# Expert weights in 2 MB units of four neighbouring rows per partition, in 8 ring slots instead of 16, with one more early unit

## The chip, the cores and the metric

The kernel runs on one core of one Trainium2 chip. The metric is the device time of one execution in microseconds (us); lower is better. The kernel before has a median of 1139.06 us over three runs (1138.79 to 1141.54).

## The reference

One layer of a streaming encoder on 256 tokens (and 16 learned ones in front), D = 1024, all in float32. A mixer of two head groups, a gated linear attention and a state-space model, comes first, then a mixture of 32 experts, each with three matrices of 1024 x 1024. Cut to what matters:

```python
mix = hybrid_mixer(h, w_in, ...)              # uses w_in (1024 x 3096) and w_out (1024 x 1024)
h = layer_norm(alpha * h + mix)
logits = h @ router_w + router_b              # top 4 of 32 experts per token
for e in range(32):                           # for the tokens x_e that chose expert e
    hid = clamped_swiglu(x_e @ w_gate[e] + b_gate[e], x_e @ w_up[e] + b_up[e])
    y_e = (hid @ w_down[e] + b_down[e]) * gate
h = layer_norm(alpha * h + sum over experts of y_e)
```

The weights of the experts are 32 x 3 x 4 MB = 384 MB (MB here is 1,048,576 bytes), and every expert's are read, whoever chose it.

## The kernel before

**Stages.** The mixer takes the first 165 us or so, the router the time to 193 us, the experts the rest. In the expert stage tokens are taken 64 at a time (a tile). `tile` (lines 946 to 992, TensorE) handles one expert:

- `hidden` for the gate matrix: the bias product of line 953, then line 959: for each of the eight row blocks `kt` of 128 rows, products of the 64 gathered tokens `xT` (the stationary operand, 64 columns) with 1024 columns of the matrix (the moving operand, two times 512). A float32 product is two instructions, so a matrix is 32 instructions.
- `scatter` of the expert before (line 942), `hidden` for the up matrix, then `gather` of the next expert's tokens (line 934): the stationary operand is a 128 x 128 piece of the token rows `xh`, read with a stride, the moving one a 0/1 matrix of 64 columns.
- four transposes of the hidden values (line 975, the same stride), two of the weights of the tokens (line 978), another `scatter`, and line 990: the down matrix.

**Weight units.** `unit_src` (line 241) cuts each matrix into four units of 256 rows. In a unit, partition p holds the rows 2p and 2p+1, which are neighbours in memory: one run of 8 KB per partition, 1 MB per unit, 12 units per expert (`UPE`). Since row 2p+k stands in partition p, the tokens have to be gathered in that order, and this is what `pair_rows` (line 254) does: for row block kt it takes every second column of `xh` or of `u_c`.

**Ring.** `ring` has 16 slots of 1 MB. The first 16 MB that it holds are the mixer's weights, 12 units of `w_in` in runs of 1 KB and 4 of `w_out`. From then on the slots are filled in order with expert units. SyncE issues all of it from one in-order program (`experts`, lines 306 to 337): before each DMA it waits until TensorE is done with the slot's last unit (for the first round the table `w_used` of line 299, afterwards the counters `unit_used`, `g_ps`, `u_ps` and `d_ps`, which TensorE raises after the eight instructions that use a unit), then issues the DMA at line 329. TensorE waits for a unit in `arrived` (line 1002).

**Early units.** The first four units of expert 28 (its gate matrix) don't pass through the ring. `load_spare` (line 302) puts them into four places in the working memory `arena` that the mixer no longer needs: two when the ring is at its thirteenth expert unit (line 318), and two after the sixteenth (line 332), one of these when the router's logits are done and one when the normalised tokens are no longer needed in transposed form. In the last round `ring_at` (line 258) skips them.

**Order of the rounds.** Four experts are written out in a loop body; the first and the last round stand outside the loop. Ahead of the last round, at expert 28, `add_residual` (line 921) adds eight products.

Of the kernel before, what the change touches and what calls it, by code (L numbers as in the profile page):

```python
# [12 lines left out]
P = 128  # L13
D = 1024
KT = D // P
# [25 lines left out]
RING = 16  # L41
UW = 2048
UPE = 3 * D * FF // (P * UW)
UNROLL = 4
ROUNDS = NE // UNROLL
SPARE = 4
# [9 lines left out]
def build(nc, x, meta, ln_in_g, ln_in_b, w_in, gla_w_a2, gla_b_a, gla_norm_g, ssd_conv_w, ssd_conv_b,  # L56
          ssd_dt_bias, ssd_a_log, ssd_d, ssd_norm_g, w_out, ln1_g, ln1_b, router_w, router_b,
          w_gate, w_up, b_gate, b_up, w_down, b_down, ln2_g, ln2_b, out):
    with ExitStack() as ctx:
# [7 lines left out]
        arena = sb("arena", [P, 19392])  # L67
# [56 lines left out]
        spare = [cut(at, 2, D) for at in (8320, 16576, 3072, 5248)]  # L124
# [77 lines left out]
        ln1_in, ln2_in, bias_in, late_in, out_done = sem("ln1_in"), sem("ln2_in"), sem("bias_in"), sem("late_in"), sem("out_done")  # L202
        landed = [sem(f"landed{s}") for s in range(RING)]
# [37 lines left out]
        def unit_src(e, u):  # L241
            m = (w_gate, w_up, w_down)[u // (UPE // 3)]
            q = u % (UPE // 3)
            rows = slice(q * 2 * P, (q + 1) * 2 * P)
            return m[0, e, rows, :].rearrange("(p k) n -> p (k n)", k=2) if isinstance(e, int) else \
                m[0, bass.ds(e, 1), rows, :].rearrange("a (p k) n -> p (a k n)", k=2)

        def slot(s):
            return ring[:, s, :].rearrange("p (k n) -> p k n", k=2)
# [17 lines left out]
        def _(sp):  # L267
# [9 lines left out]
            for n, c0 in enumerate(W_ORDER):  # L277
                sp.dma_start(ring[:, n, :].rearrange("p (k n) -> p k n", k=KT),
                             w_in[0, :, c0:c0 + 256].rearrange("(k p) n -> p k n", p=P)).then_inc(landed[n], 16)
# [14 lines left out]
            for n in range(4):  # L294
                sp.dma_start(ring[:, U_OUT + n, :].rearrange("p (k n) -> p k n", k=KT),
                             w_out[0, :, 256 * n:256 * n + 256].rearrange("(k p) n -> p k n", p=P)).then_inc(landed[U_OUT + n], 16)


            w_used = [(conv_ps, 2), (conv_ps, 4), (conv_ps, 6), (conv_ps, 8), (k_ps, 1), (v_ps, 3), (v_ps, 3), (q_ps, 1),
                      (half_used, 1), (z_ps, 2), (half_used, 2), (og_ps, 2), (wout_ps, 3), (wout_ps, 3), (wout_ps, 4), (wout_ps, 4)]  # L300

            def load_spare(q):
                sp.dma_start(unit_dst(spare[q]), unit_src(NE - UNROLL, q)).then_inc(spare_in, 16)

            def experts(it):
                first = isinstance(it, int) and it == 0
                for i in range(UPE * UNROLL):
                    at = ring_at(it, i)
                    if at is None:
                        continue  # L310
                    before = at - RING
                    if before >= 0:
                        before += i - at
                    if first and i == U_OUT:

                        sp.wait_ge(mixT_ps, 4)
                        load_spare(0)
                        sp.wait_ge(bparts_ok, 1)
                        load_spare(1)
                    if first and before < 0:  # L320
                        sp.wait_ge(*w_used[i])
                    else:
                        k, u = before // UPE, before % UPE
                        m, q = u // 4, u % 4
                        if q == 3:
                            sp.wait_ge((g_ps, u_ps, d_ps)[m], it * UNROLL + (k + 1))
                        else:
                            sp.wait_ge(unit_used, (it * UNROLL + k) * 9 + (3 * m + q + 1))
                    sp.dma_start(ring[:, at % RING, :], unit_src(it * UNROLL + i // UPE, i % UPE)).then_inc(landed[at % RING], 16)  # L329
                    if first and i == RING - 1:  # L330
                        sp.wait_ge(logit_ps, 1)
                        load_spare(2)
                        sp.wait_ge(h1_ok, NT)
                        load_spare(3)
# [4 lines left out]
            sp.wait_ge(g_ps, NE - UNROLL + 1)  # L339
# [269 lines left out]
        def _(pe):  # L609
# [9 lines left out]
            def wslot(n, kt, a=0, b=256):  # L619
                return ring[:, n, :].rearrange("p (k n) -> p k n", k=KT)[:, kt, a:b]  # L620
# [32 lines left out]
            for c in range(XC):  # L653
                n = U_XBC + c // 2
                pe.wait_ge(landed[n], 16)
# [30 lines left out]
            pe.wait_ge(landed[U_K], 16)  # L686
# [15 lines left out]
            pe.wait_ge(landed[U_V], 16)  # L702
# [28 lines left out]
            pe.wait_ge(landed[U_V + 1], 16)  # L731
# [25 lines left out]
            pe.wait_ge(landed[U_Q], 16)  # L757
# [36 lines left out]
            for hf in range(2):  # L794
                n = U_Z + hf
                pe.wait_ge(landed[n], 16)
# [45 lines left out]
            for hf in range(2):  # L842
                n = U_OG + hf
                pe.wait_ge(landed[n], 16)
# [12 lines left out]
            def out_part(t, kts, first):  # L857
                for nb in range(2):
                    b = bank[((1, 4), (2, 3))[t][nb]]
                    for kt in kts:  # L860
                        ins = mm(b[:, :], mixT[:, kt, t * P:(t + 1) * P],  # L861
                                 ring[:, U_OUT + 2 * nb:U_OUT + 2 * nb + 2, kt * 256:(kt + 1) * 256],
                                 start=first and kt == kts[0], stop=(not first) and kt == kts[-1], skip_group_check=True)
                    if not first:
                        ins.then_inc(wout_ps, 1)

            for n in range(4):
                pe.wait_ge(landed[U_OUT + n], 16)
# [60 lines left out]
            def gather(n, par):  # L929

                pe.wait_ge(sel_ok, n + 1)
                for kt in range(KT):
                    for t in range(NT):
                        ins = mm(bank[7][:, kt * SL:(kt + 1) * SL], pair_rows(xh[:, t, :], kt), sel[:, par, t, :], start=t == 0, stop=t == 1)  # L934
# [11 lines left out]
            def tile(n, par, first, unit_at, arrived, gathers, scatters):  # L946

                def hidden(m, b, free, done):
# [5 lines left out]
                    for q in range(4):  # L954
                        arrived(4 * m + q)
                        for k in range(2):
                            kt = 2 * q + k
                            for h in range(2):
                                ins = mm(b[h * SL:(h + 1) * SL, :], xT[par][:, kt, :], unit_at(4 * m + q)[:, k, h * 512:(h + 1) * 512],  # L959
                                         start=False, stop=kt == KT - 1)  # L960
                        ins.then_inc(done if q == 3 else unit_used, 1)
# [12 lines left out]
                for c in range(4):  # L974
                    ins = tr(bank[4][:, c * P:(c + 1) * P], pair_rows(u_c, c), ident[:, :])  # L975
# [9 lines left out]
                for q in range(4):  # L985
                    arrived(8 + q)
                    for k in range(2):
                        kt = 2 * q + k
                        for h in range(2):
                            ins = mm(bank[6][h * SL:(h + 1) * SL, :], hidT[:, kt % 4, (kt // 4) * SL:(kt // 4 + 1) * SL],  # L990
                                     unit_at(8 + q)[:, k, h * 512:(h + 1) * 512], start=kt == 0, stop=kt == KT - 1)
                    ins.then_inc(d_ps if q == 3 else unit_used, 1)

            def experts(it):
                for k in range(UNROLL):
                    def unit_at(u):
                        at = ring_at(it, UPE * k + u)
                        return spare[u] if at is None else slot(at % RING)

                    def arrived(u):  # L1000
                        at = ring_at(it, UPE * k + u)
                        if at is None:
                            pe.wait_ge(spare_in, 16 * SPARE)
                        else:

                            pe.wait_ge(landed[at % RING], it * (UPE * UNROLL // RING * 16) + (2 + at // RING) * 16)
# [16 lines left out]
            with pe.If(nx > 0):  # L1023
                with pe.Fori(0, nx) as i:
                    gather(i + NE, 0)
                    def arrived(u):

                        uses = 1 + (NE * UPE - SPARE + RING - 1 - u) // RING
                        pe.wait_ge(landed[u], i * 16 + (uses + 1) * 16)
                    tile(i + NE, 0, False, slot, arrived, False, False)  # L1030
# [347 lines left out]
```

## Time and profile before

| | |
|---|---|
| median of three runs | 1139.06 us |
| the profiled execution | 1139.48 us |
| its span, first to last instruction | 1137.6 us |
| mean granted TensorE clock | 0.984 of full speed |
| TensorE busy | 1095.9 us (96%) |
| VectorE, ScalarE, GpSimd busy | 231.1, 123.7, 30.7 us |
| moved by DMA | 426.96 MB (here and in all rows: million bytes), mean 375 GB/s |

The profiled execution took 1.9 us more than its span and 0.4 us more than the median. Busy shares of TensorE are modelled from pipelined instructions and don't show short waits between them; where the time goes is read from the chain of waits and from the DMA rows.

### The profile page before, as it was taken

The numbers are of one execution on the slowest core, as the hardware profiler recorded it, in microseconds if no ns is written. First come the engines' busy times: TensorE is split into PE (matmuls) and PEld (weight loads), VectorE is DVE, ScalarE is ACT, GpSimd is POOL, SyncE is SP. The second block draws the span as 40 slices with busy tenths as digits, with TensorE's granted clock in tenths as the row PEclk, the third lists the DMA queues.
The fourth block names the chain that finished last, engine by engine and source line by source line (L and its number), as shares of the span: only waits on it lengthen the run. The fifth ranks groups of instructions, "written<-read, shape, count | busy, mean of one in ns | idle before, by whom it ended". The sixth has DMA issues, their size and how long they took to land.

```text
span 1137.6 us, 13806 instructions
## 1 busy us (share of the span) xinstructions
PE 1095.9 (96%) x5600; PEld 517.9 (46%) x5600; DVE 231.1 (20%) x528; ACT 123.7 (11%) x250; POOL 30.7 (3%) x37
## 2 busy tenths in 40 slices
PE   6999998999999999999999999999999999999994
PEld 5787756444444444444444433333333333344441
DVE  4422464011111111111111111111111111111114
ACT  2241422000000000000000000000000000000001
POOL 0230002000000000000000000000000000000000
PEclk9989997899999999999999999999999999999998
DMA  8973534899999999999999999999999999999992
GB/s 260 353 302 125 170 150 157 349 411 422 421 421 420 421 421 422 421 422 421 422 422 422 422 422 422 421 423 421 422 421 423 421 422 422 422 422 421 422 419 87
DMA packets 78240, 426.96 MB, mean 375 GB/s; under 512 B 10537, under 2 KB 27026, under 8 KB 29058
## 3 DMA queue, kind: packets, MB, share of 16 engines
q1 hardware_dynamic: 76082, 423.83, 91.4%
q10 hardware_dynamic: 2128, 2.70, 0.9%
q8 instruction: 22, 0.36, 0.1%
q14 instruction: 8, 0.07, 0.0%
HBM read 425.46 MB, written 1.05 MB: 375 GB/s over the span
## 4 chain that ended last, share of the span: by engine, by line
PE 66%; DMA 29%; DVE 2%; ACT 2%; SPq 1%; issue 0%; DVEq 0%
DMA ring<-in_moe_w_up 28%; PE bank L959 26%; PE bank L990 13%; PE bank L934 7%; PE bank L942 4%; PE bank L659 3%; PE bank L861 2%; PE bank L847 1%; PE bank L799 1%; SPq L329 1%; PE bank L953 1%; PE bank L975 1%; PE bank L735 1%; PE bank L675 1%; PE bank L761 1%; PE bank L682 0%
## 5 line engine op out<-in xcount | busy, mean ns | idle before, releaser
L959 PE MATMUL bank<-ring,arena 128*64 128x512 f32 x2016 | 452.7, 596 | 13.6 <-DMA ring<-in_moe_w_up 13.6
L959 PEld LDWEIGHTS bank<-ring,arena 128*64 128x64 f32 x2016 | 139.7, 137 | 294.4 <-issue 234.5
L990 PE MATMUL bank<-ring,arena 128*64 128x512 f32 x1024 | 231.1, 604 | 0.0
L990 PEld LDWEIGHTS bank<-ring,arena 128*64 128x64 f32 x1024 | 71.7, 139 | 156.2 <-issue 137.0
L934 PEld LDWEIGHTS bank<-arena 128*128 128x128 f32 x1024 | 126.2, 200 | 25.1 <-issue 25.1
L934 PE MATMUL bank<-arena 128*128 128x64 f32 x1024 | 130.4, 287 | 0.0
L1303 DVE COPY arena<-bank 128x512 f32<-128x512 f32 x32 | 22.1, 692 | 346.3 <-PE bank L990 346.3
L1294 DVE TENSOR_SCALAR arena<-bank 128x512 f32<-128x512 f32 x32 | 22.1, 692 | 261.9 <-PE bank L959 261.9
L942 PE MATMUL bank<-arena 64*128 64x512 f32 x256 | 72.2, 642 | 0.9 <-DVE arena L1303 0.9
L576 ACT ACTIVATE arena<-arena 128x512 f32<-128x512 f32 x32 | 20.2, 631 | 465.8 <-DVE arena L1290 465.8
L1290 DVE TENSOR_SCALAR arena<-bank 128x512 f32<-128x512 f32 x32 | 22.1, 692 | 186.9 <-PE bank L959 186.9
L572 ACT ACTIVATE arena<-bank 128x512 f32<-128x512 f32 x32 | 19.1, 598 | 362.1 <-PE bank L934 362.1
L942 PEld LDWEIGHTS bank<-arena 64*128 64x128 f32 x256 | 19.4, 184 | 32.5 <-issue 32.5
L659 PE MATMUL bank<-arena,ring 128*128 128x272 f32 x128 | 30.4, 393 | 0.7 <-ACT arena L436 0.7
L861 PE MATMUL bank<-ring,arena 128*128 128x512 f32 x64 | 27.9, 593 | 0.9 <-ACT arena L430 0.9
L953 PE MATMUL bank<-arena 96*64 96x512 bf16 x128 | 25.7, 396 | 0.8 <-ACT arena L572 0.8
L659 PEld LDWEIGHTS bank<-arena,ring 128*128 128x128 f32 x128 | 23.8, 190 | 5.5 <-ACT arena L436 0.9
L975 PE MATMUL bank<-ident,arena 128*128 128x128 f32 x128 | 21.7, 292 | 2.2 <-DVE arena L1299 2.2
L1299 DVE SCALAR_TENSOR_TENSOR arena<-arena 128x512 f32<-128x512 f32 x32 | 22.2, 693 | 3.3
L953 PEld LDWEIGHTS bank<-arena 96*64 96x64 bf16 x128 | 7.3, 108 | 34.0 <-issue 34.0
L1296 DVE TENSOR_TENSOR arena<-arena 128x512 f32<-128x512 f32 x32 | 21.8, 681 | 0.0
L975 PEld LDWEIGHTS bank<-ident,arena 128*128 128x128 f32 x128 | 19.1, 218 | 3.1 <-DVE arena L1299 3.1
(242 smaller groups left out, 527.0 us busy)
## 6 DMA issues: line engine op xcount, KB each, us to landing
ring<-in_moe_w_up SPq DMA_DIRECT2D x128, 1024.0 KB, 26.2
ring<-in_moe_w_down SPq DMA_DIRECT2D x128, 1024.0 KB, 26.3
ring<-in_moe_w_gate SPq DMA_DIRECT2D x124, 1024.0 KB, 25.7
ring<-in_w_in SPq DMA_DIRECT2D x12, 1024.0 KB, 11.9
ring<-in_w_out SPq DMA_DIRECT2D x4, 1024.0 KB, 13.7
arena<-in_moe_w_gate SPq DMA_DIRECT2D x4, 1024.0 KB, 4.7
arena<-in_x SPq DMA_DIRECT2D x2, 512.0 KB, 4.7
arena<-in_ln_in_g SPq DMA_DIRECT2D x1, 512.0 KB, 10.0
```

The source lines that it names most:

```text
L659: ins = mm(bank[4 + c % 3][:, 3:3 + TOK], wslot(n, kt, (c % 2) * P, (c % 2) * P + P), hT[:, kt, :], start=kt == 0, stop=kt == KT - 1)
L861: ins = mm(b[:, :], mixT[:, kt, t * P:(t + 1) * P], ring[:, U_OUT + 2 * nb:U_OUT + 2 * nb + 2, kt * 256:(kt + 1) * 256], start=first and k ...
L934: ins = mm(bank[7][:, kt * SL:(kt + 1) * SL], pair_rows(xh[:, t, :], kt), sel[:, par, t, :], start=t == 0, stop=t == 1)
L942: ins = mm(bank[2 * t + h][:, :], selGT[h * SL:(h + 1) * SL, t * P:(t + 1) * P], y_s[h * SL:(h + 1) * SL, :], start=False, stop=False, ski ...
L953: mm(b[h * SL:(h + 1) * SL, :], oh[:, par, :], bparts[:, m, h * 512:(h + 1) * 512], start=True, stop=False)
L959: ins = mm(b[h * SL:(h + 1) * SL, :], xT[par][:, kt, :], unit_at(4 * m + q)[:, k, h * 512:(h + 1) * 512], start=False, stop=kt == KT - 1)
L975: ins = tr(bank[4][:, c * P:(c + 1) * P], pair_rows(u_c, c), ident[:, :])
L990: ins = mm(bank[6][h * SL:(h + 1) * SL, :], hidT[:, kt % 4, (kt // 4) * SL:(kt // 4 + 1) * SL], unit_at(8 + q)[:, k, h * 512:(h + 1) * 512 ...
L1290: ts(a_c, bank[4][:, :], LIMIT, None, ALU.min).then_inc(a_ok, 1)
L1294: ts(u_c, bank[5][:, :], LIMIT, -LIMIT, ALU.min, ALU.max).then_inc(u_ok, 1)
L1299: stt(u_c, u_c, 1.0, a_c, ALU.add, ALU.mult).then_inc(hid_ok, 1)
L1303: copy(y_s, bank[6][:, :]).then_inc(yd_ok, 1)
```

## The change

`UW` goes from 2048 to 4096 float32 per partition, `RING` from 16 to 8, so the ring keeps its 16 MB. A matrix is now two units of 2 MB (`UPM` = 2, `UPE` = 6). In a unit, partition p holds the rows 4p to 4p+3, one run of 16 KB. `spread_rows` takes the place of `pair_rows` and takes every fourth column. The units of the mixer's weights stay at 1 MB, two to a slot, with semaphores of their own; a slot is free for its first expert unit when both halves are used.

The scratch room that the compiler keeps for DMA descriptors is set to 1 KB per partition, and `arena` grows by 16 KB per partition. The early units are now three of 2 MB (`SPARE` = 3: the gate matrix of expert 28 and the first half of its up matrix), loaded as six halves of 1 MB in runs of 8 KB. The first two halves go to the new room of `arena` and are issued straight behind `w_out`; the four others go where the early units were, at the same points of the program.

```diff
-RING = 16
-UW = 2048
+RING = 8
+UW = 4096
+HW = UW // 2
+RPP = UW // FF
 UPE = 3 * D * FF // (P * UW)
+UPM = UPE // 3
-SPARE = 4
+SPARE = 3
-        arena = sb("arena", [P, 19392])
+        arena = sb("arena", [P, 19392 + UW])
-        spare = [cut(at, 2, D) for at in (8320, 16576, 3072, 5248)]
+        spare = [cut(at, 2, D) for at in (19392, 19392 + HW, 8320, 16576, 3072, 5248)]
...
+            m, q = (w_gate, w_up, w_down)[u // UPM], u % UPM
+            rows = slice(q * RPP * P, (q + 1) * RPP * P)
+            return m[0, e, rows, :].rearrange("(p k) n -> p (k n)", k=RPP) if isinstance(e, int) else \
+                m[0, bass.ds(e, 1), rows, :].rearrange("a (p k) n -> p (a k n)", k=RPP)
+        def half_src(e, u, j):
...
+            return m[0, e, rows, :].rearrange("(p j k) n -> p j (k n)", j=2, k=RPP // 2)[:, j, :]
...
-        def pair_rows(v, kt):
-            return v.rearrange("p (q s k) -> p q k s", s=P, k=2)[:, kt // 2, kt % 2, :]
+        def spread_rows(v, kt):
+            return v.rearrange("p (q s k) -> p q k s", s=P, k=RPP)[:, kt // RPP, kt % RPP, :]
...
+            w_used = [((conv_ps, 4),), ((conv_ps, 8),), ((k_ps, 1), (v_ps, 3)), ((q_ps, 1),), ((z_ps, 2),), ((og_ps, 2),),
+                      ((wout_ps, 3),), ((wout_ps, 4),)]
+            load_spare(0)
+            load_spare(1)
...
-                    if first and i == U_OUT:
+                    if first and i == U_OUT // 2:
                         sp.wait_ge(mixT_ps, 4)
-                        load_spare(0)
+                        load_spare(2)
                         sp.wait_ge(bparts_ok, 1)
-                        load_spare(1)
+                        load_spare(3)
...
-                    for q in range(4):
-                        arrived(4 * m + q)
-                        for k in range(2):
-                            kt = 2 * q + k
+                    for q in range(UPM):
+                        arrived(UPM * m + q)
+                        for k in range(RPP):
+                            kt = RPP * q + k
...
-                        ins.then_inc(done if q == 3 else unit_used, 1)
+                        ins.then_inc(done if q == UPM - 1 else unit_used, 1)
...
-    nc = bacc.Bacc("TRN2", target_bir_lowering=False, num_devices=1)
+    nc = bacc.Bacc("TRN2", target_bir_lowering=False, num_devices=1, dynamic_dma_scratch_size=1024)
```

## Rows read from the trace of the kernel before

**Rows 1.** The page, part 2: the span in 40 slices of 28.4 us.

```profile
DMA  8973534899999999999999999999999999999992
GB/s 260 353 302 125 170 150 157 349 411 422 421 421 420 421 421 422 421 422 421 422 422 422 422 422 422 421 423 421 422 421 423 421 422 422 422 422 421 422 419 87
```

**Rows 2.** The page, part 4: the chain that ended last, by engine.

```profile
PE 66%; DMA 29%; DVE 2%; ACT 2%; SPq 1%; issue 0%; DVEq 0%
```

**Rows 3.** The same chain in order of time: start us, us, what.

```profile
227.97 6.87 PE bank L959 x32
236.24 6.87 PE bank L959 x32
...
256.05 6.87 PE bank L959 x32
...
664.94 26.97 DMA ring<-in_moe_w_up
...
721.79 1.96 PE bank L959 x8
724.59 26.99 DMA ring<-in_moe_w_up
...
965.23 27.39 DMA ring<-in_moe_w_up
994.60 3.91 PE bank L934 x32
...
1007.32 3.63 PE bank L925 x8
1011.29 6.87 PE bank L959 x32
...
1103.77 6.90 PE bank L959 x32
```

**Rows 4.** Busy time by window: PE, PEld, DVE, ACT, POOL, granted clock, DMA share, GB/s.

```profile
85.00:90.00 5.00, 5.00 (x36) 3.26 (x36) 0.00 (x0) 0.65 (x2) 0.00 (x0) 1.00 0.00 0
190.00:195.00 5.00, 4.22 (x18) 3.09 (x19) 0.00 (x0) 1.88 (x2) 0.00 (x0) 0.50 0.00 0
215.00:220.00 5.00, 5.00 (x12) 1.51 (x12) 0.00 (x0) 0.00 (x0) 0.00 (x0) 0.68 0.68 283
220.00:225.00 5.00, 5.00 (x16) 1.37 (x14) 0.00 (x0) 0.00 (x0) 0.00 (x0) 0.64 0.47 169
240.00:300.00 60.00, 60.00 (x315) 25.54 (x312) 9.42 (x22) 4.25 (x8) 0.00 (x0) 1.00 1.01 422
```

**Rows 5.** Timeline of SyncE's queue, 220 to 229 us: start us, us issuing, count.

```profile
221.51 0.33 SPq L329 DMA_DIRECT2D ring<-in_moe_w_gate  x1
224.37 0.33 SPq L329 DMA_DIRECT2D ring<-in_moe_w_gate  x1
226.08 2.04 SPq L329 DMA_DIRECT2D ring<-in_moe_w_gate  x2
```

**Rows 6.** The DMA view of 30 to 45 us (1 KB runs), then of 240 to 1000 us.

```profile
DMA packets 5182, 5.22 MB, mean 348 GB/s; under 512 B 80, under 2 KB 5182, under 8 KB 5182
...
DMA packets 44003, 320.52 MB, mean 422 GB/s; under 512 B 4887, under 2 KB 4887, under 8 KB 4887
```

**Rows 7.** Timeline of TensorE: contiguous transposes, then the gather with its stride of two.

```profile
178.01 2.16 PE L617 MATMUL bank<-ident 128*128 128x128 f32 x18
...
243.04 3.98 PE L934 MATMUL bank<-arena 128*128 128x64 f32 x32
```

**Rows 8.** The page, part 5: weight loads of 64 and of 128 columns; the gather's matmul.

```profile
L959 PEld LDWEIGHTS bank<-ring,arena 128*64 128x64 f32 x2016 | 139.7, 137 | 294.4 <-issue 234.5
L934 PE MATMUL bank<-arena 128*128 128x64 f32 x1024 | 130.4, 287 | 0.0
L659 PEld LDWEIGHTS bank<-arena,ring 128*128 128x128 f32 x128 | 23.8, 190 | 5.5 <-ACT arena L436 0.9
```

More of the change, by code:

```diff
@@ L202, in build @@
         ln1_in, ln2_in, bias_in, late_in, out_done = sem("ln1_in"), sem("ln2_in"), sem("bias_in"), sem("late_in"), sem("out_done")
+        w_landed = [sem(f"w_landed{n}") for n in range(16)]
         landed = [sem(f"landed{s}") for s in range(RING)]
@@ L241, in unit_src, with w_unit @@
         def unit_src(e, u):
[L242 to L246, printed above, removed]
+            m, q = (w_gate, w_up, w_down)[u // UPM], u % UPM
[3 more added lines that the diff above has]
+        def half_src(e, u, j):
+            m, q = (w_gate, w_up, w_down)[u // UPM], u % UPM
+            rows = slice(q * RPP * P, (q + 1) * RPP * P)
+            return m[0, e, rows, :].rearrange("(p j k) n -> p j (k n)", j=2, k=RPP // 2)[:, j, :]
         def slot(s):
-            return ring[:, s, :].rearrange("p (k n) -> p k n", k=2)
+            return ring[:, s, :].rearrange("p (k n) -> p k n", k=RPP)
+        def w_unit(n):
+            return ring[:, n // 2, (n % 2) * HW:(n % 2 + 1) * HW].rearrange("p (k n) -> p k n", k=KT)
         def unit_dst(v):
             return v.rearrange("p k n -> p (k n)")
-        def pair_rows(v, kt):
-            return v.rearrange("p (q s k) -> p q k s", s=P, k=2)[:, kt // 2, kt % 2, :]
+        def spread_rows(v, kt):
+            return v.rearrange("p (q s k) -> p q k s", s=P, k=RPP)[:, kt // RPP, kt % RPP, :]
         def ring_at(it, i):
@@ L277, in _ @@
             for n, c0 in enumerate(W_ORDER):
-                sp.dma_start(ring[:, n, :].rearrange("p (k n) -> p k n", k=KT),
-                             w_in[0, :, c0:c0 + 256].rearrange("(k p) n -> p k n", p=P)).then_inc(landed[n], 16)
+                sp.dma_start(w_unit(n), w_in[0, :, c0:c0 + 256].rearrange("(k p) n -> p k n", p=P)).then_inc(w_landed[n], 16)
                 if n == 3:
@@ L294, in _, with load_spare @@
             for n in range(4):
[L295 to L303, printed above, removed]
+                sp.dma_start(w_unit(U_OUT + n), w_out[0, :, 256 * n:256 * n + 256].rearrange("(k p) n -> p k n", p=P)).then_inc(w_landed[U_OUT + n], 16)
+            w_used = [((conv_ps, 4),), ((conv_ps, 8),), ((k_ps, 1), (v_ps, 3)), ((q_ps, 1),), ((z_ps, 2),), ((og_ps, 2),),
+                      ((wout_ps, 3),), ((wout_ps, 4),)]
+            def load_spare(h):
+                sp.dma_start(unit_dst(spare[h]), half_src(NE - UNROLL, h // 2, h % 2)).then_inc(spare_in, 16)
+            load_spare(0)
+            load_spare(1)
             def experts(it):
@@ L331, in experts @@
                         sp.wait_ge(logit_ps, 1)
[L332 removed]
+                        load_spare(4)
                         sp.wait_ge(h1_ok, NT)
[L334 removed]
+                        load_spare(5)
             experts(0)
@@ L619, in wslot @@
             def wslot(n, kt, a=0, b=256):
-                return ring[:, n, :].rearrange("p (k n) -> p k n", k=KT)[:, kt, a:b]
+                return w_unit(n)[:, kt, a:b]
             pe.wait_ge(consts, 3)
@@ L654, in _ @@
                 n = U_XBC + c // 2
-                pe.wait_ge(landed[n], 16)
+                pe.wait_ge(w_landed[n], 16)
                 if c >= 3:
@@ L683, in meta_rows @@
                 return ins
-            pe.wait_ge(landed[U_K], 16)
+            pe.wait_ge(w_landed[U_K], 16)
             pe.wait_ge(conv, 7)
@@ L700, in _ @@
             ins.then_inc(la_ps, 1)
-            pe.wait_ge(landed[U_V], 16)
+            pe.wait_ge(w_landed[U_V], 16)
             pe.wait_ge(conv, 8)
@@ L730, in _ @@
             ins.then_inc(D_ps, 1)
-            pe.wait_ge(landed[U_V + 1], 16)
+            pe.wait_ge(w_landed[U_V + 1], 16)
             n = U_V + 1
@@ L755, in _ @@
                 ssd_update(c)
-            pe.wait_ge(landed[U_Q], 16)
+            pe.wait_ge(w_landed[U_Q], 16)
             pe.wait_ge(v_ok, 1)
@@ L795, in _ @@
                 n = U_Z + hf
-                pe.wait_ge(landed[n], 16)
+                pe.wait_ge(w_landed[n], 16)
                 for t in range(NT):
@@ L843, in _ @@
                 n = U_OG + hf
-                pe.wait_ge(landed[n], 16)
+                pe.wait_ge(w_landed[n], 16)
                 for t in range(NT):
@@ L861, in out_part @@
                         ins = mm(b[:, :], mixT[:, kt, t * P:(t + 1) * P],
-                                 ring[:, U_OUT + 2 * nb:U_OUT + 2 * nb + 2, kt * 256:(kt + 1) * 256],
+                                 ring[:, U_OUT // 2 + nb, :].rearrange("p (a k n) -> p a k n", a=2, k=KT)[:, :, kt, :],
                                  start=first and kt == kts[0], stop=(not first) and kt == kts[-1], skip_group_check=True)
@@ L867, in _ @@
             for n in range(4):
-                pe.wait_ge(landed[U_OUT + n], 16)
+                pe.wait_ge(w_landed[U_OUT + n], 16)
             pe.wait_ge(mixT_act, 2)
@@ L933, in gather @@
                     for t in range(NT):
-                        ins = mm(bank[7][:, kt * SL:(kt + 1) * SL], pair_rows(xh[:, t, :], kt), sel[:, par, t, :], start=t == 0, stop=t == 1)
+                        ins = mm(bank[7][:, kt * SL:(kt + 1) * SL], spread_rows(xh[:, t, :], kt), sel[:, par, t, :], start=t == 0, stop=t == 1)
                 ins.then_inc(gath_ps, 1)
@@ L984, in tile, with unit_at @@
                 pe.wait_ge(hidT_ok, n + 1)
[L985 to L988, printed above, removed]
+                for q in range(UPM):
+                    arrived(2 * UPM + q)
+                    for k in range(RPP):
+                        kt = RPP * q + k
                         for h in range(2):
                             ins = mm(bank[6][h * SL:(h + 1) * SL, :], hidT[:, kt % 4, (kt // 4) * SL:(kt // 4 + 1) * SL],
-                                     unit_at(8 + q)[:, k, h * 512:(h + 1) * 512], start=kt == 0, stop=kt == KT - 1)
-                    ins.then_inc(d_ps if q == 3 else unit_used, 1)
+                                     unit_at(2 * UPM + q, k)[:, h * 512:(h + 1) * 512], start=kt == 0, stop=kt == KT - 1)
+                    ins.then_inc(d_ps if q == UPM - 1 else unit_used, 1)
             def experts(it):
                 for k in range(UNROLL):
-                    def unit_at(u):
+                    def unit_at(u, r):
                         at = ring_at(it, UPE * k + u)
-                        return spare[u] if at is None else slot(at % RING)
+                        return spare[2 * u + r // 2][:, r % 2, :] if at is None else slot(at % RING)[:, r, :]
                     def arrived(u):
@@ L1002, in arrived @@
                         if at is None:
-                            pe.wait_ge(spare_in, 16 * SPARE)
+                            pe.wait_ge(spare_in, 16 * 2 * SPARE)
                         else:
-                            pe.wait_ge(landed[at % RING], it * (UPE * UNROLL // RING * 16) + (2 + at // RING) * 16)
+                            pe.wait_ge(landed[at % RING], it * (UPE * UNROLL // RING * 16) + (1 + at // RING) * 16)
                     n = it * UNROLL + k
@@ L1026, in arrived @@
                     def arrived(u):
-                        uses = 1 + (NE * UPE - SPARE + RING - 1 - u) // RING
+                        uses = (NE * UPE - SPARE + RING - 1 - u) // RING
                         pe.wait_ge(landed[u], i * 16 + (uses + 1) * 16)
-                    tile(i + NE, 0, False, slot, arrived, False, False)
+                    tile(i + NE, 0, False, lambda u, r: slot(u)[:, r, :], arrived, False, False)
                     for t in range(NT):
```

15 lines of the change are left out of this document (8 added, 7 removed).

## The prediction

> **What bounds the kernel now.** I read the slices first. From slice 9 to the last but one, DMA runs at 420 to 423 GB/s and its share is full [rows 1]; TensorE is busy there too, so the slices can't tell which of them sets the end. The chain can: 29% of it is DMA [rows 2]. In order of time it falls into three stretches [rows 3]. Up to about 630 us it is TensorE alone: gate matrices start at 227.97 and 256.05, so an expert costs TensorE 28.08 us. From 635 to 992 us nearly all of it is landings of up units. Two of these, two experts apart, are at 664.94 + 26.97 = 691.91 and 724.59 + 26.99 = 751.58, so 12 units take 29.84 us and one takes 2.486 us: DMA is 1.76 us slower per expert than TensorE, and the 16 MB in the ring cover this until 630 us. The last landing of the chain is that of expert 27's last up unit, at 965.23 + 27.39 = 992.62. From there on it is TensorE again, since expert 28's gate units came early.
>
> How much would a faster DMA give at most? With TensorE alone, expert 28's gate would start at 227.97 + 27 x 28.08 + 3.63 (line 925) = 989.8; it starts at 1011.29 [rows 3]. So 21.5 us are to be had, and no more. The end moves one for one with the landing at 992.62, as long as the delay stays above zero. I take it apart into a start, a number of units and a price. Sixteen expert units are in the ring when streaming begins, and expert 27's last up unit is number 27 x 12 + 8 = 332: 316 units are streamed, 316 x 2.486 = 785.6 us.
>
> **Longer runs.** The trace has full DMA stretches with two sizes of packet [rows 6]. At 30 to 45 us (5182 - 80) / 16 = 319 packets of 1 KB per engine took 15 us, 47.0 ns each; at 240 to 1000 us (44003 - 4887) / 16 = 2445 packets of 8 KB took 760 us, 310.8 ns each. The line through both has 0.0368 ns per byte and 9.4 ns per packet. A 16 KB packet would take 612.4 ns, against 621.6 for two of 8 KB: 1.5% less. A MB becomes 2.449 us instead of 2.486, and 316 MB cost **11.8 us less**. This goes beyond the sizes that the trace shows. The bounds: nothing, if the 422 GB/s are a limit of another kind (or the runs are cut at 8 KB), and 316 x 8 x 9.4 ns = 23.8 us if the constant vanished. I take the line, since it is the value between the two that both rows support.
>
> Of DMA the Trainium skill (DMA: Bandwidth & Descriptors, "Why small descriptors are slow") says that the engine spends about 3 fixed cycles per packet and that this matters for small ones, at 256 B; at 8 KB it would be 3 in 259 and the change would give some 0.6% of the streaming time, an estimate of about 4.6 us instead of 11.8, and the sum below would be 1140.6. The same page puts the ceiling of the fabric at 435 GB/s; the slope above, times 16 engines, comes to the same figure.
>
> **Coarser slots, at the start.** DMA is idle at 190 to 195 us, and again within 215 to 225 us, where it moves 283 and 169 GB/s [rows 4]: every slot is full, and SyncE waits for expert 0's down matrix, on which TensorE works at half clock. The first two quarters come free for issues at 221.51 and 224.37 [rows 5]. The stream as a whole starts at the issue time less the time of the units before it: 221.51 - 8 x 2.486 = 201.6, 224.37 - 9 x 2.486 = 202.0, 226.08 - 10 x 2.486 = 201.2; the latest counts, 202.0. With 2 MB slots the first down unit is free only when both quarters are: 224.37 - 4 x 4.898 = 204.8. So the start is **2.8 us later**. By 240 us the rate is 422 [rows 4], so no later gap.
>
> **Coarser units, at the end.** After a landing TensorE had 8 instructions to do, 1.96 us [rows 3]; now 16, half of a 6.87 us matrix plus the same start: 3.7 us. **1.7 us more**, once, behind expert 27's up matrix. In the experts before it this is hidden, as DMA goes on meanwhile: 7 of 8 slots are in flight then.
>
> **Stride of four instead of two.** This touches `gather` (32 instructions) and line 975 (4). The spacing of its instructions is set by the 128-column loads. Contiguous: (2.16 - 0.28) / 17 = 111 ns; stride two: (3.98 - 0.28) / 31 = 119 ns [rows 7] (0.28 us, about the 287 ns of one [rows 8], is the duration of the last). A stride of two costs 8 ns per load. No row shows a stride of four. Bounds: nothing, and one more full read of the columns; loads of 64 and 128 columns differ by 190 - 137 = 53 ns [rows 8], so 106 ns more for each of 36 loads, 3.8 us per expert. I take another 8 ns, nearest to the row: 0.3 us per expert. It counts where TensorE sets the pace: four gathers behind expert 27's up, **1.2 us**. Before them it is under the DMA.
>
> **Edits at nothing.** The early unit more: 2 MB, 5 us of DMA, put into the queue ahead of the first expert unit; idle time such as 85 to 90 us [rows 4] takes it. It doesn't shorten the stream up to expert 27, as it belongs to expert 28. Behind it there was slack already: expert 31's last up unit landed at about 992.62 + 44 x 2.486 = 1102.0 and was needed at 1103.77 + 5.15 = 1108.9 [rows 3]. The slack grows by 5 us and nobody waits for it; without that cover it would be worth those 5 us. The descriptor scratch: all weight DMAs are SyncE's; I find no user, cost from 0 to 0. Half as many issues and waits: SyncE and `arrived` are not late; 0. The slots' merged first waits (slot 2 on `v_ps`): all of them are in before tile 0, as the idle 190 to 195 shows; 0, and if one were late it would delay tile 0 by the 5 us of a unit at most.
>
> **Sum.** -11.8 + 2.8 + 1.7 + 1.2 = -6.1 us on the profiled 1139.5 gives 1133.4; the median stands 0.4 below the profiled execution: **1133.0 us**. The landing would be at 983.6, and of the 21.5 us of delay some 12.5 remain, less what the gathers take from it.
>
> **Rivals.**
>
> (a) *The gather becomes the bound.* Without DMA waits the end is 1139.5 - 21.5 + 32p, with p the added TensorE time per expert. At p = 0.67 us this is the time of before: 19 ns per load. With p = 3.8 it is 1240 us, 8.9% slower. For it: the loads are the bound of the gather already, and stride two is 8 ns dearer than none. Against: that is only 7%, at twice as many places in memory touched. The Trainium skill (SBUF — State Buffer, the note on cachelines under the port swizzle) says that lines have 16 bytes and that two hits per line are wanted to hide the access; a stride of four float32 has one. By that rule this rival holds. A load takes 0.83 ns per column (53 / 64 [rows 8]) while a moving operand takes 6.87 / 32 / 512 = 0.42, so a load has twice the time per line; this is why I give it only 0.2.
>
> (b) *Longer runs give nothing.* 422 GB/s stays: 1139.5 + 2.8 + 1.7 + 1.2 = 1145.2, median 1144.8, 0.5% slower. It includes the case that the packets are cut at 8 KB. The point from which it decides is a gain of 5.7 us, half of the line's. For it: the rate is flat to 1% in all slices. Chance 0.15.
>
> (c) *In between*: p from 0.55 to 0.75 us (1139.5 - 21.5 + 32p = 1135.6 to 1142), or a third to two thirds of the line's gain (4 to 8 us: 1141.2 to 1137.2). Some 1136 to 1142 us, chance 0.13. The skill's estimate above would fall here.
>
> (d) *More than the line gives*, down to the floor without any DMA wait, 1139.5 - 21.5 + 32 x 0.3 = 1127.6: chance 0.05.
>
> The forecast has 0.47, with 1129 to 1135.5 as its own range. **Numbers.** A measurement of this kernel tells about 0.3%, 3.4 us, from no change. Faster: forecast, (d) and a little of (c), 0.55. Same: most of (c), 0.13. Slower: (a), (b), 0.32. The range goes from 1128 over (b) and the lower part of (a), to 1160.
>
> **What would show it.** Right: 16 KB packets, about 51,000 packets in all instead of 78,240; slices at 428 GB/s; the chain's last DMA landing near 984 us; expert 28's gate about 7 us earlier than 1011.29; the gather at 4.0 to 4.3 us instead of 3.98. Wrong: slices at 422 (b); a gather of over 4.7 us and a chain with no DMA behind 250 us (a); a DMA gap of more than 5 us at 215 to 235 us; the last DMA landing of the chain behind expert 28.

## The result and the profile after

The changed kernel takes **1306.5 us** (median of four runs, 1304.1 to 1309.8) against 1139.4 for the kernel before on the same chips: a ratio of 1.1465, 95% interval 1.1433 to 1.1496, 167 us slower. The forecast was 1133.0, the range up to 1160. The page of the changed kernel, lines of parts 1 to 5:

```profile
span 1302.2 us, 13282 instructions
...
PEclk9989987899999888888888888888899999888888
DMA  8963556898988888888888888898998888856850
GB/s 272 358 261 135 161 194 258 357 383 369 374 367 368 367 367 366 363 367 366 365 364 368 365 366 365 365 379 380 387 382 364 366 367 367 365 236 255 369 248 33
DMA packets 51023, 426.94 MB, mean 328 GB/s; under 512 B 7513, under 2 KB 24002, under 8 KB 26034
...
PE 96%; DVE 2%; ACT 1%; DMA 0%; issue 0%; DVEq 0%
...
L947 PEld LDWEIGHTS bank<-arena 128*128 128x128 f32 x1024 | 241.4, 328 | 25.3 <-issue 25.3
...
L947 PE MATMUL bank<-arena 128*128 128x64 f32 x1024 | 247.3, 411 | 0.0
```

The packets are as announced, 51,023. Nothing else is as forecast. DMA has gone from the chain (0%, it was 29% [rows 2]), and its rate in the slices has fallen from 422 GB/s [rows 1] to about 367: it no longer sets the pace, the ring is full and DMA waits for TensorE. The gather, line 947 here, is busy for 247 us in all instead of 130, 411 ns per instruction instead of 287 [rows 8]. And the granted clock averages 0.904, where it was 0.984. One expert in the chain that ended last (start us, us, what):

```profile
744.74 6.87 PE bank L972 x32
751.61 1.06 PE bank L955 x4
752.67 0.34 PE bank L966 x2
753.00 6.87 PE bank L972 x32
759.87 7.66 PE bank L947 x32
767.53 0.85 PE bank L988 x4
768.39 0.43 PE bank L991 x2
768.81 2.01 PE bank L955 x4
770.82 7.83 PE bank L1003 x32
...
778.87 6.87 PE bank L972 x32
```

Gate matrices start at 744.74 and 778.87, 34.13 us apart instead of 28.08 [rows 3]. The gate and up matrices take 6.87 us as they did. The same part of an expert in the kernel before, in its chain: the gather, the two groups of transposes, the second scatter and the down matrix:

```profile
299.25 3.91 PE bank L934 x32
303.16 0.51 PE bank L975 x4
303.67 0.22 PE bank L978 x2
303.89 1.06 PE bank L942 x4
304.95 7.02 PE bank L990 x32
```

So of the 6.05 us (6.06 by these rounded rows), 3.75 are the gather. 0.21 + 0.95 + 0.81 = 1.97 are instructions that the change doesn't touch: they run after the clock has fallen. So do the four transposes of the hidden values, which the change does touch; question 5 shows that their 0.34 is the clock too and not the stride, which makes 2.31 us of clock. Windows of 1 us within the gather (columns as in [rows 4]):

```profile
763.00:764.00 1.00, 1.00 (x6) 1.00 (x6) 0.00 (x0) 0.00 (x0) 0.00 (x0) 1.00 0.96 410
766.00:767.00 1.00, 1.00 (x6) 1.00 (x5) 0.00 (x0) 0.00 (x0) 0.00 (x0) 0.50 0.92 393
```

In the first the clock is at its upper level (2.4 GHz), in the second at the lower one (1.2 GHz); it falls about 6 us into the slow loads and comes back in the down matrix. The gather itself does as many instructions per us at either level, so it isn't the clock that slows it. Nor is it DMA traffic beside it: the very first gather of the changed kernel, at 184.92 us, takes 7.68 us although DMA moves nothing from 188 us on; in the kernel before it took 6.73, both at a clock of about 0.5.

### The profile page after: what moved, and what is told of

Same layout as the page of the kernel before. It is cut to its first block, busy times and chain, and to the rows that moved or that the text cites. A ratio compares the mean times of both kernels' runs of the same rounds, so it can differ in the third digit from the quotient of the medians.

```text
span 1302.2 us, 13282 instructions
## 1 busy us (share of the span) xinstructions
PE 1273.3 (98%) x5600; PEld 658.9 (51%) x5600; DVE 231.0 (18%) x528; ACT 126.3 (10%) x250; POOL 30.7 (2%) x37
## 4 chain that ended last, share of the span: by engine, by line
PE 96%; DVE 2%; ACT 1%; DMA 0%; issue 0%; DVEq 0%
PE bank L972 34%; PE bank L1003 19%; PE bank L947 19%; PE bank L955 7%; PE bank L672 2%; PE bank L874 2%; PE bank L988 2%; PE bank L966 1%; PE bank L860 1%; PE bank L812 1%; PE bank L991 1%; PE bank L748 1%; PE bank L930 1%; PE bank L774 1%; PE bank L688 1%; PE bank L695 0%
## 5 line engine op out<-in xcount | busy, mean ns | idle before, releaser
L972 PE MATMUL bank<-ring,arena 128*64 128x512 f32 x2000 | 442.3, 595 | 0.0
L972 PEld LDWEIGHTS bank<-ring,arena 128*64 128x64 f32 x2000 | 141.1, 137 | 269.7 <-issue 265.0
L947 PEld LDWEIGHTS bank<-arena 128*128 128x128 f32 x1024 | 241.4, 328 | 25.3 <-issue 25.3
L1003 PE MATMUL bank<-ring,arena 128*64 128x512 f32 x1024 | 250.3, 644 | 0.0
L947 PE MATMUL bank<-arena 128*128 128x64 f32 x1024 | 247.3, 411 | 0.0
L1003 PEld LDWEIGHTS bank<-ring,arena 128*64 128x64 f32 x1024 | 75.1, 150 | 194.7 <-issue 194.7
L955 PE MATMUL bank<-arena 64*128 64x512 f32 x256 | 101.0, 877 | 0.9 <-DVE arena L1316 0.9
L955 PEld LDWEIGHTS bank<-arena 64*128 64x128 f32 x256 | 25.8, 244 | 37.6 <-issue 37.6
L988 PE MATMUL bank<-ident,arena 128*128 128x128 f32 x128 | 33.9, 418 | 2.2 <-DVE arena L1312 2.2
L988 PEld LDWEIGHTS bank<-ident,arena 128*128 128x128 f32 x128 | 28.2, 256 | 3.1 <-DVE arena L1312 3.1
## 6 DMA issues: line engine op xcount, KB each, us to landing
ring<-in_moe_w_up SPq DMA_DIRECT2D x63, 2048.0 KB, 11.6
```

Of the source, the lines that this page charges most:

```text
L947: ins = mm(bank[7][:, kt * SL:(kt + 1) * SL], spread_rows(xh[:, t, :], kt), sel[:, par, t, :], start=t == 0, stop=t == 1)
L955: ins = mm(bank[2 * t + h][:, :], selGT[h * SL:(h + 1) * SL, t * P:(t + 1) * P], y_s[h * SL:(h + 1) * SL, :], start=False, stop=False, ski ...
L988: ins = tr(bank[4][:, c * P:(c + 1) * P], spread_rows(u_c, c), ident[:, :])
```

## The experiments

The theory after reading this profile, **S**: reading the stationary operand with a stride of four columns doubles the load, and the clock falls behind it; the rest of the change does what the prediction said. The rival **D**: the 16 KB runs or the 2 MB slots slow TensorE or the transfers. Six questions, nine runs.

**1. The change without its stride.** In the changed kernel:

```diff
-            return v.rearrange("p (q s k) -> p q k s", s=P, k=RPP)[:, kt // RPP, kt % RPP, :]
+            return v.rearrange("p (q s k) -> p q k s", s=P, k=2)[:, kt // 2, kt % 2, :]
```

> The changed kernel with one edit: the stationary operands of the gather and of the hidden values' transposes are read with a stride of two columns again, as before the change, instead of four. (The tokens' columns then no longer go with the rows of the 2 MB units, so the products are of other pairs.) Theory S (the stride of four doubles the 128-column loads, and the clock falls behind them; nothing else in the change costs much): the gather is back at 3.98 us, the clock at 0.98, and the time is what the prediction's other terms give, 1139.5 - 11.8 + 2.8 + 1.7 = 1132 us, 1129 to 1136. Rival D (the 16 KB runs or the 2 MB slots slow TensorE or the transfers themselves): most of the 167 us stays, over 1200 us. Rival of the packets: slices stay at 422 GB/s and the time is about 1144 us.

Measured: 1128.8 us, ratio 0.9915 (0.9900 to 0.9929), 9.8 us faster than the kernel before (six runs from 1127.3 to 1131.2; the profiled one is the 1131.2). The slices of its page, and its chain around expert 28:

```profile
GB/s 261 353 343 151 126 167 193 297 415 424 428 428 427 428 427 427 429 428 428 428 428 429 427 429 429 429 428 429 428 428 429 428 429 428 429 427 428 428 364 38
```

```profile
949.14 35.18 DMA ring<-in_moe_w_up
...
984.36 3.65 PE bank L972 x16
988.02 3.91 PE bank L947 x32
...
1004.70 6.87 PE bank L972 x32
```

428 GB/s, and the last landing at 949.14 + 35.18 = 984.3. S stands, D falls: with the 16 KB runs and the 2 MB slots in place, the loss of 167 us is gone. (What the slots alone cost, some 3 us, is in question 6.)

**2. The stride without the change.** In the kernel before, `pair_rows` takes every fourth column:

```diff
-            return v.rearrange("p (q s k) -> p q k s", s=P, k=2)[:, kt // 2, kt % 2, :]
+            return v.rearrange("p (q s k) -> p q k s", s=P, k=4)[:, kt // 4, kt % 4, :]
```

> The kernel before with one edit: the same operands are read with a stride of four columns (again products of other pairs), units, slots and runs as before. Theory S: TensorE alone sets the pace, 34.1 us per expert as in the changed kernel, gather 7.7 us, clock about 0.90, 1295 to 1310 us. Rival D: the stride costs little by itself, under 1180 us.

Measured: 1305.4 us, ratio 1.1464 (1.1447 to 1.1481), the same ratio as the change. Its page and the end of its chain:

```profile
PEclk9989987889888888888888888888999999888888
```

```profile
1246.93 7.66 PE bank L934 x32
1255.87 2.01 PE bank L942 x4
1257.88 7.79 PE bank L990 x32
```

One line of address pattern accounts for all of the loss.

**3. No stride at all.** The changed kernel with `return v[:, kt * P:(kt + 1) * P]`.

> The changed kernel with those operands read without any stride (products of other pairs). Theory S, with DMA setting the pace: TensorE saves a further 8 ns on each of 36 loads in the four experts behind the last DMA wait, about 1 us less than with a stride of two: 1129 to 1135 us, a gather of 3.6 to 3.8 us. If TensorE rather than DMA sets the pace with a stride of two, it saves some 9 us against that run instead.

Measured: 1126.3 us, ratio 0.9893 (0.9878 to 0.9907), 2.5 us less than with a stride of two and below the 1129 to 1135 expected. Gather 3.71 us in its chain. It still waits for DMA up to expert 27 (last landing 980.3), so TensorE doesn't set the pace. The landing is 4.0 us earlier than in the run with a stride of two, and the traces show where 3.0 of these arise: at the start of the stream. There expert 0's down matrix takes 7.02 us at full clock instead of 9.90 at mostly half clock, and the first down unit is free for the issue at 222.19 us instead of 225.16. That the contiguous loads keep the clock up there isn't shown; both profiled runs without a stride have the 7.02, the four with a stride of two (the kernel before among them) 8.31 to 9.90.

**4. Which strides are slow?** One kernel, each expert of the unrolled loop with a stride of its own; the indices are `v[:, kt:kt + 127 * s + 1:s]`:

```diff
+                if step == 0:
+                    for kt in range(KT):
+                        for t in range(NT):
+                            ins = mm(bank[7][:, kt * SL:(kt + 1) * SL], strided(xh[:, t, :], kt, 1), sel[:, par, t, :], start=t == 0, stop=t == 1)
...
```

> The kernel before, with the gather's stationary operand read at a stride of 1, 2, 3 and 4 columns by position in the unrolled loop of four experts (products of other pairs; the transposes keep their stride of two). Theory S1, two reads per line of 16 bytes are enough: 3.6, 3.98, then a step; a stride of three (on average 1.33 reads per line) takes two thirds or all of the way to 7.5 us. Theory S2, cost by bytes stepped over: steady growth, 3.7, 4.0, 5.8, 7.6. Theory S3, only strides of 16 bytes and more are slow: a stride of three is as short as two, about 4.0, and four is 7.5. As one expert in four has the slow gather, the whole takes about 1150 us.

Measured, in one execution: 1193.4 us. The 32 instructions of the gather in its chain, strides 2, 3, 4 and 1 in this order:

```profile
486.00 3.95 PE bank L942 x32
...
514.10 6.06 PE bank L946 x32
...
546.72 7.66 PE bank L950 x32
...
580.90 3.72 PE bank L938 x32
```

The first loads of strides three and four in its timeline, at full clock:

```profile
514.89 1.49 PEld L946 LDWEIGHTS bank<-arena 128*128 128x128 f32 x8
...
546.86 1.26 PEld L950 LDWEIGHTS bank<-arena 128*128 128x128 f32 x5
```

At a stride of three two of them take 0.44 us in the timeline and eight take 1.49, so they are (1.49 - 0.44) / 6 = 175 ns apart; at a stride of four two take 0.56 us and five 1.26, so (1.26 - 0.56) / 3 = 233 ns. In lines of 16 bytes the four strides touch 32, 64, 96 and 128 per load. 64, 96 and 128 lines at 1.83 ns are 117, 176 and 234 ns; the contiguous load, 32 lines, stays at 111, 0.87 ns for each of its 128 columns. None of S1, S2 and S3 had this law; S2 comes nearest for strides up to four. (The 6.06 us at a stride of three include a stretch at half clock; 32 loads at 175 ns are 5.6.) The whole time was above the 1150 expected, for two reasons: the stride of three is slow too, and I had left out the clock, which in the chain falls behind the strides of three and four and not behind one and two. There it adds some 2.4 us each time (down matrix, second scatter and both groups of transposes), 38 us in all if it does so in every round, an estimate.

A second kernel separates lines from bytes, and asks whether the moving operand suffers too:

> The kernel before with two probes (products of other pairs; the residual's eight instructions ahead of the last round are replaced). First, the gather's stationary operand at strides of 5, 6, 7 and 8 columns by position in the loop. The runs so far gave 111, 118, 175 and 234 ns per load at strides of 1 to 4: the last three are 64, 96 and 128 lines of 16 bytes times 1.83 ns. Theory L (a read costs 1.83 ns per line, or 0.83 ns per column where that is more): all four strides read 128 lines, 234 ns each at full clock. Rival B (cost by the bytes stepped over): 290 to 470 ns. Second, a moving operand of 512 columns at strides of 1, 2 and 4 (lines 924, 926, 928), four products of two instructions each, spaced 213 ns at a stride of 1. Theory L: 256 and 512 lines, 470 and 940 ns per instruction. Rival M (only weight loads suffer): 213 ns for all three.

Its gathers in the timeline of TensorE, strides 6, 7, 8 and 5:

```profile
520.77 7.40 PE L944 MATMUL bank<-arena 128*128 128x64 f32 x32
554.84 7.65 PE L948 MATMUL bank<-arena 128*128 128x64 f32 x32
589.06 7.88 PE L952 MATMUL bank<-arena 128*128 128x64 f32 x32
623.36 7.31 PE L940 MATMUL bank<-arena 128*128 128x64 f32 x32
```

Eight instructions each with a moving operand of 512 columns at strides 1, 2 and 4:

```profile
1154.14 3.70 PE L924 MATMUL bank<-arena,tri 128*128 128x512 f32 x8
1157.67 3.76 PE L926 MATMUL bank<-arena,tri 128*128 128x512 f32 x8
1161.28 7.36 PE L928 MATMUL bank<-arena,tri 128*128 128x512 f32 x8
```

Strides of five to eight cost about what four does (7.2 to 7.8 us in the chain against 7.66, where a cost by bytes would have given 9.3 us and more): it is lines, not bytes, and theory L holds. It doesn't explain the 8% by which these four strides differ. The moving operand suffers too, so rival M falls. Less the duration of the last one (0.59, 0.61 and 1.06 us) and over seven gaps, they are 444, 450 and 900 ns apart, where L gave 470 and 940 for strides of two and four. My base was wrong there: 213 ns is about the spacing with a stationary operand of 64 columns (32 in 6.87 us), and with 128 columns it is 444 ns, probably because the two halves of 64 are worked on side by side, which no run tests. A stride of two costs 2% and a stride of four doubles, 1.76 ns per line.

**5. Loads and clock apart.** The changed kernel, gather cut in two:

```diff
+                if gathers:
+                    gather(n + 1, 1 - par, range(0, 4))
                 hidden(1, bank[5], u_ok, u_ps)
                 if gathers:
-                    gather(n + 1, 1 - par)
+                    gather(n + 1, 1 - par, range(4, 8))
```

> The changed kernel, whole computation, stride of four, with the gather cut in two: its first 16 products ahead of the up matrix and its last 16 behind it. It tells the two costs of the slow loads apart. If the fall of the clock comes from the 7.5 us of slow loads in one piece, it goes: 28.07 + 32 x (0.234 - 0.118) + 4 x 0.11 = 32.2 us per expert, the clock at 0.98 and 1139.5 - 21.5 + 32 x 4.15 = 1251 us. If the clock falls all the same, 1290 us or more.

Measured: 1281.6 us (1270.5 to 1283.0), ratio 1.1235 (1.119 to 1.128), mean clock 0.947 instead of 0.904. The up matrix (32 instructions), the transposes of the hidden values and the half gathers in two neighbouring experts of its timeline:

```profile
710.19 9.60 PE L973 MATMUL bank<-ring,arena 128*64 128x512 f32 x32
...
723.50 0.68 PE L991 MATMUL bank<-ident,arena 128*128 128x128 f32 x4
...
740.55 3.95 PE L947 MATMUL bank<-arena 128*128 128x64 f32 x16
...
744.67 7.03 PE L973 MATMUL bank<-ring,arena 128*64 128x512 f32 x32
751.63 3.94 PE L947 MATMUL bank<-arena 128*128 128x64 f32 x16
```

It lies between the two expectations. Cutting the slow stretch in two spares 25 us, and since the loads are the same I put all of it down to the clock. But the clock still falls in most experts, in 13 of the 15 between 414 and 900 us in the chain, for a shorter time and not always in the same place (in the first line, 9.60 instead of 7.03 us, it is in the up matrix). What decides when it falls was not settled.

Since the fall moves about, this run also shows the four transposes with their stride of four at full clock, the second line: 0.68 us. In the first probe of question 4, where they have a stride of two, the same four take 0.68 us at full clock (489.78 us) and 1.06 at half clock (519.96 us). So the stride of four costs the transposes nothing that is seen here, and the 0.34 us of the changed kernel are the clock. Without them the first expectation is 4 x 0.11 x 32 = 14 us lower, 1237; the measured time stays between the two.

**6. The other terms.** The coarser slots without the longer runs: the whole computation, two DMAs with 8 KB runs per slot, `pair_rows` as before.

```diff
-                    sp.dma_start(ring[:, at % RING, :], unit_src(it * UNROLL + i // UPE, i % UPE)).then_inc(landed[at % RING], 16)
+                    for j in range(2):
+                        sp.dma_start(ring[:, at % RING, j * HW:(j + 1) * HW], half_src(it * UNROLL + i // UPE, i % UPE, j)).then_inc(landed[at % RING], 16)
```

> 2 MB slots as in the change, but each is filled by two DMAs of 1 MB in runs of 8 KB, two rows per partition, and the operands have a stride of two: the whole computation is done. It has the coarser slots without the longer runs. By the prediction's terms: slices at 422 GB/s and 2.8 + 1.7 = 4.5 us more than the kernel before, 1143 us; against the run with stride two and 16 KB runs (1128.8), 11.8 us more, 1140.6. Rival: the coarser slots are what brought the 9.8 us, and it stays near 1129 us.

Measured: 1141.5 us, ratio 1.0029 (1.0017 to 1.0042), 3.3 us more than before. Page, and the chain at the last landing:

```profile
GB/s 262 355 333 148 138 171 173 332 422 422 421 421 421 420 422 422 422 421 422 422 420 423 422 421 422 422 422 422 422 422 422 421 422 423 421 422 421 421 391 38
```

```profile
994.65 3.65 PE bank L969 x16
```

422 GB/s again, and the landing 2.0 us later than the 992.62 of before [rows 3]. The slots cost, and the runs give: against the run with a stride of two it lands 10.3 us later, and takes 10.3 us more by the profiled executions, 12.7 by the medians.

The third early unit: run 1 with `SPARE = 2`.

> The run with a stride of two (1128.8 us) with two early units instead of three, in the four old places. Prediction: the third one serves expert 28's up matrix, for which nobody waits: the same to within 1 us, 1128 to 1130. Rival: it shortens the stream, and without it the time is 2.45 x 2 = 4.9 us longer, about 1133.7 us.

Measured: 1131.0 us, ratio 0.9929 (0.9909 to 0.9949), 1 us above the 1128 to 1130 expected. The interval overlaps that of the run with three, and the last landing is at 983.86 instead of 984.32. The early unit doesn't shorten the stream; by the two intervals a difference in the end of up to some 4 us can't be excluded, though the lowest and the highest of the six times (1127.6 and 1132.0) are only 0.3 and 0.8 us above those of the other six.

**A version that keeps the gain.** The order of the columns can be put right once, instead of at each load:

```diff
+                for q in range(2):
+                    ins = nc.scalar.activation(xp[:, t, q * 512:(q + 1) * 512].rearrange("p (k s) -> p k s", k=RPP),
+                                               xh[:, t, q * 512:(q + 1) * 512].rearrange("p (s k) -> p k s", k=RPP), ACT.Copy)
...
-                stt(u_c, u_c, 1.0, a_c, ALU.add, ALU.mult).then_inc(hid_ok, 1)
+                stt(hp.rearrange("p (k s) -> p s k", k=RPP), u_c.rearrange("p (s k) -> p s k", k=RPP), 1.0,
+                    a_c.rearrange("p (s k) -> p s k", k=RPP), ALU.add, ALU.mult).then_inc(hid_ok, 1)
```

> 2 MB units and 16 KB runs as in the change, but the columns are put in the order of the rows once: ScalarE copies the tokens' rows into a permuted buffer before the first gather, and VectorE writes the hidden values permuted, so both kinds of load read contiguous columns. The early units are two again, since the buffer takes the new room. The whole computation is done. Theory S (only the strided loads cost): the time of the run without stride, 1126.3, plus at most 2 us for the copy ahead of the first gather: 1125 to 1130 us. Rival: VectorE's strided write or the copy on ScalarE is slow enough to be waited for (hidden values later than the gather, first gather later): 1131 us or more.

Measured: **1126.4 us**, ratio 0.9898 (0.9881 to 0.9916), 1.0% faster than the kernel before with the whole computation. Its chain behind the last landing, and VectorE's permuted write in its groups by line:

```profile
982.57 3.65 PE bank L979 x16
986.22 3.72 PE bank L954 x32
989.94 0.44 PE bank L995 x4
```

```profile
L1319 DVE SCALAR_TENSOR_TENSOR arena<-arena 128x512 f32<-128x512 f32 x32 | 33.7, 1054 | 3.3
```

The permuted write takes 1054 ns instead of 693, and ScalarE's copies took 1.1 us each for 512 columns; the first gather starts at 188.1 us in its chain, 2.3 us later than in the kernel before. The permuted write is covered by the gather: the transposes (line 995) start at 989.94, when it ends. The copies don't show in the medians (1126.4 against 1126.3 with no stride and no copy), but they do in the profiled executions: the first down unit is issued at 224.82 instead of 222.19, the last landing is at 982.52 instead of 980.30, and the end is 2.6 us later. A copy that is done before the first gather needs it would be worth up to that.

## Why the prediction was wrong

- **The failed step** is "Stride of four instead of two", in its words: "I take another 8 ns, nearest to the row: 0.3 us per expert." Measured: 115 ns more per load of the gather, 3.75 us for its 32, and nothing for the transposes; and that in every expert, since TensorE then sets the pace throughout, and not in four of them. The upper bound that I had put there, one more full read of the columns, 106 ns, was nearly exact (its 3.8 us are for 36 loads, of which only the 32 of the gather turned out slower). I extended two points (111 and 119 ns at strides one and two) as if the cost grew with the stride. It is the larger of two limits, one per column and one per line, and the second overtakes the first just below a stride of two: the 8 ns were not a small slope but the foot of a steep one.
- **Rival (a)** is what happened, with a chance of 0.2. Its price of 1240 us was the loads' alone. Here the forecast lacked a second mechanism altogether: the clock falls behind the slow loads in nearly every expert, 2.31 us of other work per expert. The sum with the measured terms is 1139.5 - 21.5 + 32 x (3.75 + 2.31) = 1312, against 1304.1 for the profiled execution. It counts 32 full experts, where the last has no gather and the clock falls less in the first ones and in the last (down matrices of 7.02 to 7.49 us in experts 1 to 3, 7.04 in expert 31).
- **The Trainium skill's rule** (SBUF — State Buffer, the note on cachelines: lines of 16 bytes, two hits per line wanted) was right, and the traces agree: two reads per line cost 5%, one costs double. The same note adds that 4 float32 can be strided for free; if that means a stride of four, the 234 ns against 111 contradict it. I argued the rule away: "a load has twice the time per line". But the moving operand that I compared with was read beside a stationary operand of 64 columns; beside one of 128 it takes 444 / 512 = 0.87 ns per column, as long as a load's, so the factor of two that I relied on wasn't there.
- **Longer runs: right.** 428 GB/s, as the line through 1 KB and 8 KB gave; 11.8 us forecast; 10.3 lie between the landings with 16 KB and with 8 KB runs (questions 1 and 6), though the stream with 16 KB started 1.3 us later (first down unit issued at 225.16 instead of 223.85), so the runs themselves gave 11.6. The 3 cycles per packet of the Trainium skill (DMA: Bandwidth & Descriptors, "Why small descriptors are slow") would have given 4.6 by the estimate in the prediction and don't hold here; the 9.4 ns of the rows do.
- **Coarser slots and units: right in kind**, 2.0 (landings of question 6 and before) and 3.65 - 1.96 = 1.7 us against 2.8 and 1.7. The last landing without the stride, 984.3, was forecast at 983.6.
- **Early unit, scratch, fewer waits at nothing**: borne out within what the runs can tell; the scratch and the merged waits were not tried alone.
- **The sum without the failed step** was 1139.5 - 11.8 + 2.8 + 1.7 = 1132.2 for the profiled execution, which took 1131.2. The landing came 0.7 us later than forecast, and the last down matrix took 7.04 us where the profiled execution before had 8.47, a gain that is no term of the sum. The median, 1128.8, is 3 us below the sum; other executions than the profiled one have no trace, so this stays open.

## What to carry to other kernels

A layout that lengthens DMA runs moves the price into the address patterns of the engines that read it: before costing such a change, count the 16-byte lines that each read touches, not the stride. Where two rows give a trend, ask which limit each of them shows; a row that sits just above a flat part is the place where the other limit can begin. And price a slow stretch of TensorE twice: what it takes itself, and what the work behind it takes if the clock falls (here 3.75 and 2.31 us per expert). The order can often be put right once, by an engine with time to spare.

## What was not expected of the hardware

- In float32, at full clock, each weight load of the gather, of 128 columns, takes the larger of 111 ns and 1.83 ns per 16-byte line touched: 111, 119, 175, 233 ns at strides of 1 to 4, and about as much beyond, up to 8 (7.2 to 7.8 us per 32). A moving operand of 512 columns keeps the same shape: 3.70, 3.76 and 7.36 us for eight instructions at strides of 1, 2 and 4. The transposes do not: four of them take 0.44 us in the chain without a stride (question 3) and 0.51 or 0.52 at strides of 2 and 4, at full clock. Why they differ wasn't looked into.
- The load with a stride of four is not slower at 1.2 GHz than at 2.4: six instructions per us at either. Those with strides of one and two are: the first gather, at a clock of about 0.5, takes 6.73 us with either, and 3.71 and 3.91 us at full clock. So at half clock a stride of four costs little: 7.68 us there.
- TensorE was busy without a gap by the profile (whose busy time is modelled), and its clock fell all the same, in nearly every expert, when the loads before were slow. With the slow stretch cut in two it fell in most of them still, and the time was 25 us shorter.
- At 16 KB the packets still gain on 8 KB, 428 GB/s against 422.
